# Banded attention: masks added by VectorE in float32 instead of by identity products of TensorE

## What is computed

```python
def sliding_window_gqa(q, k, v, sinks):
    ...
    scores = jnp.einsum('bnqhgd,bnkhd->bnhgqk', qb, kb).astype(jnp.float32) * (HEAD_DIM ** -0.5)
    ...
    in_band = (lag >= 0) & (lag < WINDOW)
    valid = in_band[None] & ((blk > 0) | (kj >= WINDOW)[None])
    scores = jnp.where(valid[None, :, None, None], scores, NEG_INF)
    ...
    probs = jax.nn.softmax(jnp.concatenate([scores, sink], axis=-1), axis=-1)[..., :-1]
    out = jnp.einsum('bnhgqk,bnkhd->bnqhgd', probs.astype(v.dtype), vb)
```

## Time and profile before

| | |
|---|---|
| time, median of 3 runs | 2794.56 us (2794.47 to 2798.0) |
| the profiled execution | 2794.62 us, of which the span is 2792.8 us |
| PE busy | 2730.1 us, 98% of the span |
| DVE busy | 1952.5 us, 70% |
| ACT busy | 1383.3 us, 50% |
| POOL busy | 58.2 us, 2% |
| HBM read | 249.57 MB, 90 GB/s with the writes |

### The profile page before, as it was taken

How to read it: one execution, slowest core, us unless ns; L and a number is a source line. 1 busy time by engine, 2 the same in 40 slices (tenths; PEclk the granted TensorE clock), 3 DMA queues, 4 the chain that set the end, 5 groups by cost and what they waited for, 6 DMA issues and landing times. The chain is left out here.

```text
span 2792.8 us, 51007 instructions
## 1 busy us (share of the span) xinstructions
PE 2730.1 (98%) x21244; PEld 2413.5 (86%) x21244; DVE 1952.5 (70%) x2715; ACT 1383.3 (50%) x2115; POOL 58.2 (2%) x45
## 2 busy tenths in 40 slices
PE   8999999999999999999999999999999998999998
PEld 7999888778999888999888777999888877888887
DVE  6887855676887776886856777788785369655641
ACT  4445544554545455544545555444556367544430
POOL 1000000001000001000000000100000000000000
PEclk9999999999999999999999999999999999999999
DMA  4334311103233331334122103133422211322331
GB/s 150 107 106 174 103 49 61 40 3 121 84 106 125 117 136 46 100 105 177 64 83 76 55 3 114 63 105 106 159 98 99 69 44 35 114 83 98 98 122 52
DMA packets 71076, 254.95 MB, mean 91 GB/s; under 512 B 7672, under 2 KB 8696, under 8 KB 70848
## 3 DMA queue, kind: packets, MB, share of 16 engines
q1 hardware_dynamic: 70848, 251.70, 26.6%
HBM read 249.57 MB, written 2.10 MB: 90 GB/s over the span
## 5 line engine op out<-in xcount | busy, mean ns | idle before, releaser
L261 PE MATMUL ps<-h_hi,w_space 128*128 128x512 f32 (+1 forms) x2624 | 698.3, 351 | 3.3 <-DVE h_lo L367 3.3
L271 PE MATMUL ps<-w_space 128*128 128x512 f32 x2448 | 567.3, 391 | 1.3 <-PEq L91 0.8
L271 PEld LDWEIGHTS ps<-w_space 128*128 128x128 f32 x2448 | 457.7, 188 | 95.8 <-issue 1.2
L261 PEld LDWEIGHTS ps<-h_hi,w_space 128*128 128x128 f32 x2624 | 463.2, 190 | 70.3 <-DVE h_lo L367 4.2
L249 DVE TENSOR_TENSOR w_space<-w_raw,w_space 128x1024 fp32r<-128x1024 f32 x256 | 312.0, 1231 | 254.4 <-ACT w_space L241 254.2
L261 PE MATMUL ps<-h_lo,w_space 128*128 128x512 f32 (+1 forms) x1312 | 457.9, 349 | 0.0
L950 PE MATMUL ps<-h_hi,w_space 128*128 128x256 f32 x2432 | 450.8, 283 | 0.0
L950 PEld LDWEIGHTS ps<-h_hi,w_space 128*128 128x128 f32 x2432 | 385.3, 192 | 0.2
L241 ACT CAST w_space<-w_raw 128x1024 fp32r<-128x1024 f32 x256 | 265.0, 1047 | 189.0 <-PE ps L261 102.9
L950 PE MATMUL ps<-h_lo,w_space 128*128 128x256 f32 x1216 | 344.6, 283 | 0.0
L261 PEld LDWEIGHTS ps<-h_lo,w_space 128*128 128x128 f32 x1312 | 249.8, 190 | 29.8 <-issue 0.5
(11 more groups left out here) (467 smaller groups left out, 3737.0 us busy)
## 6 DMA issues: line engine op xcount, KB each, us to landing
w_raw<-in_w_ffn_in SPq DMA_DIRECT2D x176, 512.0 KB, 3.4
w_raw<-in_w_in SPq DMA_DIRECT2D x64, 512.0 KB, 3.5
w_raw<-in_w_ffn_out SPq DMA_DIRECT2D x56, 512.0 KB, 3.4
w_raw<-in_w_up SPq DMA_DIRECT2D x44, 512.0 KB, 3.4
row_blocks<-in_w_ffn_out SPq DMA_DIRECT2D x8, 2048.0 KB, 12.0
w_raw<-in_w_out SPq DMA_DIRECT2D x24, 512.0 KB, 4.0
w_raw<-in_w_down SPq DMA_DIRECT2D x22, 512.0 KB, 3.5
w_raw<-in_w_ple_gate SPq DMA_DIRECT2D x16, 512.0 KB, 3.9
```

Of the source, the lines that this page charges most:

```text
L261: m = nc.tensor.matmul(c.ps[:, bank, t], part[:, cols], moving[:, k, t], start=(opens and k == 0 and i == 0), stop=(k == KD - 1 and i == 2 ...
L271: m = nc.tensor.matmul(c.ps[:, bank + half, :], x, part[:, half * S:(half + 1) * S], start=(first and i == 0), stop=(final and i == 2), sk ...
```

## The change

The identity products go, and with them `ident_r` and its copy by ScalarE. The masks are kept in float32 (`kept_masks`), and VectorE adds them in two places. In `maxima`, one reduction over both banks becomes four instructions, one for each query block, that add the mask, write the sum to a scratch tile (`biased`) and give its maximum, with the sink's logit as the start value; each waits for the one before it. In the new `mask_scores`, VectorE adds the mask to the exact scores on their way from PSUM to `probs`, in three instructions, and ScalarE then exponentiates `probs` in place. `mask_scores` is called last in `vector_after` behind tile 2h+7. ScalarE's `exponents` waits for it (`masked`) where it waited for the scores (`scored`).

```diff
     def rough_scores(self, pe, nc, h):
...
-            mask = self.masks_r[:, 0:2, :] if b == 0 else self.masks_r[:, 1:2, :].to_broadcast([P, 2, 2 * WIN])
-            nc.tensor.matmul(c.ps[:, bank, :], self.ident_r[:, :], mask, start=True, stop=False)
             for n in (2 * b, 2 * b + 1):
...
-                                     self.k_hi[:, h // GROUP, first * P:(n + 1) * P], start=False, stop=(n % 2 == 1))
+                                     self.k_hi[:, h // GROUP, first * P:(n + 1) * P], start=True, stop=True)
     def scores(self, pe, nc, h):
         c = self.c
         if h:
-            pe.wait_ge(self.exps, 2 * h)
+            pe.wait_ge(self.masked, 2 * h)
...
-            nc.tensor.matmul(c.ps[:, bank, :], self.ident_r[:, :], self.masks_r[:, 2:3, :].to_broadcast([P, 2, 2 * WIN]),
-                             start=True, stop=False)
...
     def exponents(self, act, nc, h):
...
         for b in range(2):
-            act.wait_ge(self.scored, 2 * h + b + 1)
-            if h:
-                act.wait_ge(self.pv_done, h)
-            w = S - b * P
-            nc.scalar.activation(self.probs[:, 2 * b:2 * b + 2, :].rearrange("p j q -> p (j q)")[:, 0:w],
-                                 c.ps[:, self.SCORE_BANK + b, 0:w], ACT.Exp, scale=self.SCALE).then_inc(self.exps, 1)
+            act.wait_ge(self.masked, 2 * h + b + 1)
+            probs = self.probs_of(b)
+            nc.scalar.activation(probs, probs, ACT.Exp, scale=self.SCALE).then_inc(self.exps, 1)
...
     def maxima(self, dve, nc, h):
...
-        first = c.ps[:, self.FIRST_BANK:self.FIRST_BANK + 2, :].rearrange("p b (n k) -> p (b n) k", n=2)
-        nc.vector.tensor_reduce(self.top[:, h % 2, :], first, AX, ALU.max).then_inc(self.rough_read, 1)
-        dve.wait_ge(self.rough_read, h + 1)
...
+        for n in range(NT):
+            first = WIN if n == 0 else 0
+            at = (n % 2) * 2 * WIN
+            if h or n:
+                dve.wait_ge(self.rough_read, NT * h + n)
+            nc.vector.tensor_tensor_reduce(out=self.biased[:, first:], in0=c.ps[:, self.FIRST_BANK + n // 2, at + first:at + 2 * WIN],
+                                           in1=self.kept_masks[:, min(n, 1), first:], scale=1.0, scalar=self.sinks[:, h:h + 1],
+                                           op0=ALU.add, op1=ALU.max,
+                                           accum_out=self.top[:, h % 2, n:n + 1]).then_inc(self.rough_read, 1)
+        dve.wait_ge(self.rough_read, NT * (h + 1))
...
-        nc.vector.tensor_scalar(self.neg_top[:, h % 2, :], self.top[:, h % 2, :], self.sinks[:, h:h + 1], -1.0, ALU.max,
-                                ALU.mult).then_inc(self.tops, 1)
+        nc.vector.tensor_scalar(self.neg_top[:, h % 2, :], self.top[:, h % 2, :], -1.0, None, ALU.mult).then_inc(self.tops, 1)
...
+    def mask_scores(self, dve, nc, h):
+
+        c = self.c
+        mask = self.kept_masks[:, 2:3, :].to_broadcast([P, 2, 2 * WIN])
+        for b in range(2):
+            dve.wait_ge(self.scored, 2 * h + b + 1)
+            if h:
+                dve.wait_ge(self.pv_done, h)
+            scores = c.ps[:, self.SCORE_BANK + b, :].rearrange("p (j q) -> p j q", j=2)
+            probs = self.probs[:, 2 * b:2 * b + 2, :]
+            if b == 0:
+                nc.vector.tensor_tensor(probs, scores, mask, ALU.add).then_inc(self.masked, 1)
+            else:
+                nc.vector.tensor_tensor(probs[:, 0, :], scores[:, 0, :], self.kept_masks[:, 2, :], ALU.add)
+                nc.vector.tensor_tensor(probs[:, 1, 0:WIN], scores[:, 1, 0:WIN], self.kept_masks[:, 2, 0:WIN],
+                                        ALU.add).then_inc(self.masked, 1)
...
     def vector_after(self, dve, nc, n):
...
             if h + 2 < HEADS:
                 self.rest_of_q(dve, nc, h + 2)
+            self.mask_scores(dve, nc, h)
```

More of the change, by code:

```diff
@@ L1778, in __init__ @@
         self.exps, self.sink_exps, self.pv_done = st.sem("exps"), st.sem("sink_exps"), st.sem("pv_done")
-        self.summed, self.inverted, self.normed = st.sem("summed"), st.sem("inverted"), st.sem("normed")
+        self.masked = st.sem("masked")
+        self.shared, self.normed = st.sem("shared"), st.sem("normed")
         self.transposed, self.out_copied = st.sem("transposed"), st.sem("out_copied")
@@ L1831, in scores @@
                     nc.tensor.matmul(o, k[:, h // GROUP, j * P:(j + 1) * P], self.q_both[:, h % 3, j * P:last * P],
-                                     start=False, stop=False)
+                                     start=(k is self.k_hi), stop=False)
                 if j == 0:
                     pe.wait_ge(self.diag_ready, h + 1)
-                m = nc.tensor.matmul(o, self.ones_r[:, :], self.diag[:, j:last, :], start=False, stop=(j % 2 == 1))
+                m = nc.tensor.matmul(o, self.ones_r[:, :], self.diag[:, j:last, :], start=False, stop=True)
             m.then_inc(self.scored, 1)
@@ L1919, in scalar_after @@
             act.wait_ge(c.consts_loaded, 48)
-            nc.scalar.copy(self.ident_r[:, :], c.mat["ident"]).then_inc(self.consts, 1)
             nc.scalar.copy(self.ones_r[:, :], c.mat["ones"]).then_inc(self.consts, 1)
@@ L1923, in scalar_after @@
             act.wait_ge(self.loaded, 16)
-            nc.scalar.copy(self.masks_r[:, :, :], self.masks).then_inc(self.consts, 1)
+            nc.scalar.copy(self.kept_masks[:, :, :], self.masks).then_inc(self.consts, 1)
         if n == 5:
@@ L1991, in maxima, with probs_of @@
                                 ALU.mult).then_inc(self.diag_ready, 1)
+    def probs_of(self, b):
+        return self.probs[:, 2 * b:2 * b + 2, :].rearrange("p j q -> p (j q)")[:, 0:S - b * P]
+    def mask_scores(self, dve, nc, h):
[3 more added lines that the diff above has]
+            dve.wait_ge(self.scored, 2 * h + b + 1)
+            if h:
+                dve.wait_ge(self.pv_done, h)
[3 more added lines that the diff above has]
+                nc.vector.tensor_tensor(probs, scores, mask, ALU.add).then_inc(self.masked, 1)
+            else:
+                nc.vector.tensor_tensor(probs[:, 0, :], scores[:, 0, :], self.kept_masks[:, 2, :], ALU.add)
+                nc.vector.tensor_tensor(probs[:, 1, 0:WIN], scores[:, 1, 0:WIN], self.kept_masks[:, 2, 0:WIN],
+                                        ALU.add).then_inc(self.masked, 1)
     def normalise(self, dve, nc, h):
@@ L1998, in normalise @@
         nc.vector.tensor_tensor(self.share[:, h % 2, :, :], o[:, :, DH:DH + 1], self.sink_exp[:, h % 2, :, :],
[L1999 to L2002, removed]
+                                ALU.add).then_inc(self.shared, 1)
+        dve.wait_ge(self.shared, 2 * h + 1)
+        nc.vector.reciprocal(self.share[:, h % 2, :, :], self.share[:, h % 2, :, :]).then_inc(self.shared, 1)
+        dve.wait_ge(self.shared, 2 * h + 2)
         if t:
```

13 lines of the change are left out of this document (6 added, 7 removed).

## The result

The changed kernel takes 2801.61 us (median of 16 runs) against 2795.07 us before, run beside it: a ratio of 1.0022, 95% interval 1.0015 to 1.0029, so 4 to 8 us slower. One of the 16 runs took 2972.12 us at a granted clock of 0.85 and is left out of the ratio. The profiled execution took 2801.64 us, 7.02 more than that of before. Forecast were 2801.7 us. The total was right, but two of its parts were not, and they cancelled.

What follows compares the result with a forecast made beforehand. TensorE bounds the stage, VectorE's added work being free only where it was early. Per layer, 7.4 us saved go on six waits and a late end, leaving +3.55; two layers +7.1 on 2794.62 give 2801.7 us, range 2794 to 2814.

Steps and rivals of the forecast that it cites:

- The saving: TensorE loses four identity products a head, 0.46 us ahead of rough scores, 0.23 per exact bank: 7.4 us a layer.
- The maximum: VectorE's four add-and-maximum instructions between rough scores and diag: 2.2 us instead of 1.22, 0.92 more per head.
- The four are cheap: Rival: a maximum of 1.66 to 2.0 us, waits and savings cancel, 2796 to 2799; chance 0.28.
- the prediction's own case: A maximum of 2.2 us with waits at named places: 2801.7 us, by itself 2799 to 2805; chance 0.34.
- The upper bound of 3.5: VectorE's maximum taking two passes per column, as a scan does: 3.5 us; as a rival 2816, chance 0.08.
- The additions: VectorE's three mask additions to the exact scores, behind its other work of tile 2h+7: 1.27 us per head.
- The places: TensorE waits at diag of heads 0, 6, 7, values of heads 0, 1, rough scores 6: 0.6 to 2.3 us.
- the 0.6 at head 7: At diag of head 7, TensorE comes at 527.87 and waits 0.6 us for VectorE, ready at 528.45.
- the walk: Following TensorE through one layer, time shifts from place to place, ending 3.55 us later; 1.35 with a maximum of 1.66.
- The end: Stage end: last exponentials 4.95 us later, less ScalarE's 1.40 idle ahead of its copy-out: 3.55 us later a layer.
- The clock: Rival: TensorE's clock falls to half in a long wait, 3 to 6 us on top, 2805 to 2808; chance 0.25.
- the prediction's own signs of being wrong: A maximum under 1.9 us, waits at heads 2 to 5, granted clock 0.50 inside the stage, or change outside it.

Runs made afterwards that it cites:

- x6_unmasked_max: Kernel before with no masks in the rough scores, maximum over all 256 keys; exact scores keep identity products: 2790.56 us, ratio 0.9978.
- x7_hybrid: Kernel before without masks in the rough scores, VectorE adding the exact scores' masks for heads 0 to 3 alone: 2785.43 us, ratio 0.9963.
- x9_three_engines: Kernel before, rough scores unmasked; exact masks: VectorE heads 0-3, TensorE 4-5, GpSimd 6-7; head 0's maximum ahead of tile 9's weights: 2782.62 us, ratio 0.9955.
- x3_filler: The whole change plus nine unused TensorE products ahead of the wait for diag of head 6: 2803.96 us, ratio 1.0030.
- x12_relief_pool: The change reordered on VectorE and ScalarE, exact scores of heads 4 and 5 keeping identity products, GpSimd's factor multiplications held until L2236's product: 2786.32 us, ratio 0.9970.
- x11_order_pool: The change with its instructions reordered on VectorE and ScalarE, GpSimd's four factor multiplications held back until L2236's product is done: 2788.11 us, ratio 0.9975.
- x8_pool: Kernel before, rough scores unmasked; exact masks not added, GpSimd multiplies the exponentials by 1 or 0 instead: 2783.76 us, ratio 0.9958.

## Why the prediction was right

- **The saving** stands: 0.46 us for each half of a head. Built from such steps, x6_unmasked_max was to gain 2.8 us a layer and gained 3.1 and 3.2, x7_hybrid 1.6 more and gained 1.6, x9_three_engines 1.8 more and gained 1.6 and 1.7.
- **The maximum was mis-sized**: 1.97 us instead of 2.2, and with the shorter change of sign (170 ns for 229 before) 0.7 more per head instead of 0.92. The column write lasts 0.083, as forecast, but under the end of its add-and-maximum, so that a pair takes 0.53 us where the sum had 0.60. So the maximum lies at the upper edge of the rival *The four are cheap* (1.66 to 2.0 us), not in the prediction's own case. The upper bound of 3.5 was too high for its own row: two passes at the scan's pace with the other terms make some 3.2.
- **The additions** were right: from 421.12 to 422.33 (422.05 and 0.28) at head 0, 1.21 instead of 1.24; the exponentials in place take 1.05 for the pair.
- **The places** were right, all but the last: waits of 1.61, 1.09, 0.83, 1.82 and 2.29 us against 1.9, 1.6, 0.9, 2.3 and 2.3, none at heads 2 to 5. Four of them are 0.1 to 0.5 shorter than forecast, and the 0.6 at head 7 did not come. The smaller maximum is only a part of that. At the values of head 0 it brings TensorE forward as much as VectorE; what shortened that wait is that VectorE's last work ahead of the additions (L1964) ended 0.19 us later than before, counted from the start of the stage, and not 0.92. The gaps of some 0.5 us behind `diag` mostly closed, and the walk had let none of them close. The wait at `diag` of head 6 did not shrink, though the walk's maximum was too long there too: the weights ahead of it took 1.80 us instead of 1.21 beside GpSimd (508.25 to 509.54), and the walk had given GpSimd no price. No run takes GpSimd away at that place, so this part is argued from the row:

```profile
508.82 1.80 DVE L249 TENSOR_TENSOR w_space<-w_raw,w_space 128x1024 fp32r<-128x1024 f32 x1
```

- **The end** was forecast 3.55 us late per layer and came 3.45 and 3.29 late, of which the fall of the clock is 1.4 each.
- **The clock** was the rival with 0.25, and it came true at one wait in each stage, 1.4 us each; a granted clock of 0.50 inside the stage was one of the prediction's own signs of being wrong. Without it the change is 3.9 us slower, 2799.0, the upper edge of the cheap rival, and my own case had said 7.1 without it. Interpolated between the prediction's ends (1.35 a layer at 1.66, 3.55 at 2.2), a maximum of 1.97 gives about 2.6 a layer; measured without falls were 2.0 and 1.8. So the walk was too dear by some 1.6 us a layer, about 0.95 of it through the maximum and the rest not divided (the gaps that closed may be a part of it), and the clock that it had kept apart gave 1.4 back. The mechanism was right, a late VectorE at named places; that 2801.6 came out to 0.1 us was luck, the cheap rival and the clock's rival together.

What stays open: whether the clock falls behind a given wait. It fell behind 1.59 us ahead of rough scores 6 in x3_filler, and not behind 1.59 and 1.82 there in the change; behind 1.61 at `diag` of head 0 in one stage of x12_relief_pool, and not behind the same wait in its other stage or in the change; and in x11_order_pool's first stage behind 0.74 and 0.95 close together. The rows read here do not tell them apart.

## What to carry to other kernels

When work moves from a full engine to one that is 70% busy, price it where the other engine is late, not by its mean share: here two moves that were worth -3.3 and +1.1 us alone cost 6.7 together, 3.9 without the falls of the clock, because they spend the same idle time. Give each mask to the engine that has time at that head, and ask first whether it is needed at all. Before an instruction is brought forward, see what it releases: six exponentials moved ahead set GpSimd free beside the one VectorE product that TensorE waited for.

## What was not expected of the hardware

A fall of the granted clock to 0.50 costs 0.9 (x3_filler) to 1.8 us (x12_relief_pool) of a stage where a stage without it stands beside it, 1.4 at `diag` of head 6, and the runs scatter with it: of 28 runs of the kernel before, beside the first four experiments, the fastest took 2788.87 us at a mean granted clock of 0.999, and the four at 0.995 took 2797.0 to 2799.7. Differences of a few us are therefore read more surely from the length of the stage than from a few runs' time. And GpSimd's multiplications, of no weight in the page (2% busy), double a VectorE instruction with both inputs in SBUF (686 to 1505 ns in x8_pool), but do not lengthen one that reads PSUM (687 and 684 ns).
